# A two-block transformer kernel: small projection weights loaded by another queue, half of an early piece asked for sooner, router logits in two banks

## The reference

```
h = x + hybrid_mixer(rmsnorm(x), w_in, ...)          # delta rule heads, pooling, w_out
probs = softmax(rmsnorm(h) @ router_w)               # 16 experts
gate, idx = top_k(probs.T, 32)                       # each expert picks 32 tokens
h = h + scatter_add(gate * ((silu(xg @ w_gate[e]) * (xg @ w_up[e])) @ w_down[e]))
x2 = rmsnorm(h, norm_final)                          # end of block one
proj = rmsnorm(x2, norm_mix_2) @ w_in_2              # block two
(qa, ka, va, q_idx, k_idx, w_idx, qb, kb, vb, gdown, ogate) = split(proj)
   # sizes 512 512 512 256 32 8 256 256 512 16 512
x3 = x2 + concat(sparse_attention(...), gated_linear_attention(...)) @ w_out_2
y  = rmsnorm(x3 + ffn(rmsnorm(x3)))
```

## Time and profile before

| | |
|---|---|
| median of 3 runs | 1424.22 us (1423.8 to 1425.07) |
| the profiled execution | 1424.23 us |
| its span, first to last instruction | 1422.4 us |
| mean granted TensorE clock | 0.899 of full |
| HBM read | 475.88 MB, 335 GB/s over the span |
| TensorE, DVE, ACT, POOL busy | 77%, 26%, 22%, 22% |

### The profile page before, as it was taken

How to read it: one execution, slowest core, us unless ns; L and a number is a source line. 1 busy time by engine, 2 the same in 40 slices (tenths; PEclk the granted TensorE clock), 3 DMA queues, 4 the chain that set the end, 5 groups by cost and what they waited for, 6 DMA issues and landing times.

```text
span 1422.4 us, 19705 instructions
## 1 busy us (share of the span) xinstructions
PE 1092.7 (77%) x8358; PEld 629.3 (44%) x8358; DVE 369.9 (26%) x755; ACT 305.9 (22%) x457; POOL 307.7 (22%) x216
## 2 busy tenths in 40 slices
PE   7999997556756656666575665666678999999998
PEld 7998732111211211211031121121125988999997
DVE  6586530000100001000010010000104857553333
ACT  5753210000000000000000000000004636454443
POOL 6796000000000000000000000000003785386661
PEclk9999999888877888888888888888899999999999
DMA  9513999999999999999999999999999832575540
GB/s 288 186 34 121 389 425 428 427 428 427 428 428 428 429 428 428 429 428 429 428 428 429 429 428 428 428 429 427 428 428 330 220 119 92 178 249 178 178 149 30
DMA packets 95288, 478.06 MB, mean 336 GB/s; under 512 B 11098, under 2 KB 64217, under 8 KB 70393
## 3 DMA queue, kind: packets, MB, share of 16 engines
q1 hardware_dynamic: 94528, 476.30, 83.2%
q10 hardware_dynamic: 697, 0.84, 0.2%
HBM read 475.88 MB, written 1.25 MB: 335 GB/s over the span
## 4 chain that ended last, share of the span: by engine, by line
DMA 57%; PE 40%; DVE 2%; ACT 1%; issue 0%; SPq 0%; DVEq 0%; ACTq 0%
PE bank L1321 21%; DMA ring<-in_expert_w_down 20%; DMA ring<-in_expert_w_up 18%; DMA ring<-in_expert_w_gate 18%; PE bank L1024 4%; PE bank L2113 4%; PE bank L1046 2%; PE bank L410 1%; PE bank L427 1%; DMA ring<-in_w_in 1%; PE bank L1061 1%; PE bank L423 1%; PE bank L1515 0%; PE bank L1496 0%; PE bank L442 0%
## 5 line engine op out<-in xcount | busy, mean ns | idle before, releaser
L1024 PE MATMUL bank<-ring,work 128*32 128x512 f32 x2000 | 306.2, 745 | 201.6 <-DMA ring<-in_expert_w_up 124.4
L1024 PEld LDWEIGHTS bank<-ring,work 128*32 128x32 f32 x2000 | 60.5, 123 | 435.6 <-DMA ring<-in_expert_w_up 200.4
L1295 POOL TENSOR_TENSOR slot_r<-ring,slot_r 128x512 fp32r<-128x512 f32 (+1 forms) x123 | 226.8, 1873 | 102.5 <-ACT slot_r L1267 102.4
L1304 POOL TENSOR_TENSOR slot_r<-ring,slot_r 128x512 fp32r<-128x512 f32 x16 | 21.9, 1392 | 956.3 <-ACT slot_r L1273 956.3
L1046 PE MATMUL bank<-ring,work 128*32 128x512 f32 x1024 | 155.3, 741 | 85.8 <-DMA ring<-in_expert_w_down 81.0
L1321 PE MATMUL bank<-slot_r 128*128 128x256 f32 (+2 forms) x1080 | 160.5, 288 | 3.8 <-DVE tokm_r L2475 1.8
L1321 PEld LDWEIGHTS bank<-slot_r 128*128 128x128 f32 (+1 forms) x1080 | 145.2, 192 | 8.0 <-issue 5.3
L1098 DVE TENSOR_TENSOR work<-work,bank 128x512 f32<-128x512 f32 x16 | 11.0, 688 | 491.2 <-PE bank L1024 491.2
L1321 PE MATMUL bank<-work_r,slot_r 128*128 128x256 f32 x704 | 129.1, 283 | 0.2 <-DVE chan_r L1836 0.2
L1108 DVE SCALAR_TENSOR_TENSOR hres<-bank,work,hres 128x512 f32<-128x512 f32 x64 | 48.1, 751 | 276.0 <-PE bank L1061 272.8
L1267 ACT ACTIVATE slot_r<-ring 128x2048 fp32r<-128x2048 f32 x62 | 116.7, 1904 | 3.2 <-DMA ring<-in_w_in 3.2
(11 more groups left out here) (419 smaller groups left out, 1046.6 us busy)
## 6 DMA issues: line engine op xcount, KB each, us to landing
ring<-in_expert_w_down SPq DMA_DIRECT2D x64, 2048.0 KB, 35.7
ring<-in_expert_w_gate SPq DMA_DIRECT2D x63, 2048.0 KB, 36.0
ring<-in_expert_w_up SPq DMA_DIRECT2D x62, 2048.0 KB, 35.8
ring<-in_w_in SPq DMA_DIRECT2D x23, 1024.0 KB, 8.2
ring<-in_w_ffn_gate SPq DMA_DIRECT2D x11, 1024.0 KB, 5.7
ring<-in_w_ffn_up SPq DMA_DIRECT2D x11, 1024.0 KB, 5.4
ring<-in_w_ffn_down SPq DMA_DIRECT2D x11, 1024.0 KB, 4.9
ring<-in_w_out SPq DMA_DIRECT2D x8, 1024.0 KB, 5.0
```

The source lines that it names most:

```text
L1024: ins = pe.matmul(bank[b][32 * j:32 * j + 32, :], xg[:, 2 * s + kk, a * CAP:(a + 1) * CAP], w_[kk][:, j * W5:(j + 1) * W5], start=(s == 0 ...
L1295: ins = eng.tensor_tensor(ring_r[s][:, a:a + step], ring[:, s, a:a + step], ring_r[s][:, a + UNIT:a + UNIT + step].bitcast(F32), ALU.subtract)
L1304: ins = eng.tensor_tensor(ring_r[s][:, at:at + q], ring[:, s, at:at + q], ring_r[s][:, at + UNIT:at + UNIT + q].bitcast(F32), ALU.subtract)
```

## The change

Four edits:

1. The three loads of the small weights leave `second_sync` and slot 7. ACT issues them, in the last pair at its first expert (a = 0, expert 14), after that expert's gate products are done and ahead of its Silu (`small_weights`, signal `rel_in`). They go into `work0`. ACT makes `kgw_hi` and DVE `kgw_lo` in expert 15, between hT and the copies to `yo`; ACT waits for the loads there (`rel_in` 80), DVE for ACT (`act_chain` 4). SP no longer waits for them ahead of the bias rows. Two Square scratch places move, since `kgw` now lies in `work0`.
2. The `masks` half of the mask piece is issued right after pieces 2 and 3 instead of behind piece 5; the `work0` half stays where it was.
3. The logits of token tile t go into bank 2 or 5, with a signal each; DVE takes the maximum and its scaling for each tile by itself, and ACT's first Exp waits for the first tile's alone.
4. Counts of `SLOT_LOADS` and `ROUTED` follow.

```diff
-SLOT_LOADS["ffn"] = [n + m for n, m in zip(SLOT_LOADS["second"], (3, 3, 3, 3, 3, 2, 0, 19))]
+SLOT_LOADS["ffn"] = [n + m for n, m in zip(SLOT_LOADS["second"], (3, 3, 3, 3, 3, 2, 0, 16))]
...
-                    ins = pe.matmul(bank[2][:, t * E:(t + 1) * E], chan[:, k, t * P:(t + 1) * P], rw[:, k, :],
+                    ins = pe.matmul(bank[LOGITS[t]][:, 0:E], chan[:, k, t * P:(t + 1) * P], rw[:, k, :],
                                     start=(k == 0), stop=(k == DK - 1))
-            ins.then_inc(S.route_out, 1)
+                ins.then_inc(S.route_out, 1)
...
-                act.wait_ge(S.lmax_ready, 2)
+                act.wait_ge(S.lmax_ready, t + 1)
...
-            link(dve.tensor_reduce(lmax, bank[2][:, 0:TT * E].rearrange("p (t e) -> p t e", t=TT), AX.X, ALU.max))
-            dve.scalar_tensor_tensor(lmax, lmax, -1.0, rs, ALU.mult, ALU.mult).then_inc(S.lmax_ready, 2)
+            for t, done in enumerate(("first", "logits")):
+                dve.wait_ge(S.route_out, ROUTED[done])
+                link(dve.tensor_reduce(lmax[:, t:t + 1], bank[LOGITS[t]][:, 0:E], AX.X, ALU.max))
+                dve.scalar_tensor_tensor(lmax[:, t:t + 1], lmax[:, t:t + 1], -1.0, rs[:, t:t + 1], ALU.mult, ALU.mult)\
+                    .then_inc(S.lmax_ready, 1)
...
             for a in range(PAIR):
                 act.wait_ge(S.slot_used, SPE * (PAIR * i + a) + 4)
+                if last and a == 0:
+                    small_weights(act)
                 act.activation(sg, bank[GB][:, :], ACT.Silu).then_inc(S.silu_ready, 1)
...
                 if last and a == PAIR - 1:
                     act.activation(warm, eps, ACT.Sqrt)
+                    act.wait_ge(S.rel_in, 80)
+                    act.activation(kgw_hi, kgw_w, ACT.Copy).then_inc(S.act_chain, 1)
...
+        def small_weights(act):
+            w3 = io["w_in_2"].rearrange("o (k p) c -> (o p) k c", p=P)
+            for at, c, w in ((0, KI, IDX_DIM), (IDX_DIM, GD, GATE_RANK), (IDX_DIM + GATE_RANK, WI, IDX_HEADS)):
+                act.dma_start(kgw_w[:, :, at:at + w], w3[:, :, c:c + w]).then_inc(S.rel_in, 16)
...
                 if last and a == PAIR - 1:
+                    dve.wait_ge(S.act_chain, 4)
+                    dve.tensor_tensor(kgw_lo, kgw_w, kgw_hi.bitcast(F32), ALU.subtract).then_inc(S.chan_ready, 1)
                     dve.wait_ge(S.slot_used, SPE * E)
...
             for n in freed:
                 sp.wait_ge(*freed[n])
                 load_slot(sp, 0, n)
+                if n == 3:
+                    load_slot(sp, 0, MASK_PIECE, True)
...
-kgw_w = ring[:, 7, 3072:3072 + DK * KGW].rearrange("p (k c) -> p k c", k=DK)
-kgw_lo, kgw_hi = (ring_r[7][:, 3072 + i * DK * KGW:3072 + (i + 1) * DK * KGW].rearrange("p (k c) -> p k c", k=DK)
-                  for i in range(2))
+kgw_w = work0[:, 11 * W5:11 * W5 + DK * KGW].rearrange("p (k c) -> p k c", k=DK)
+kgw_lo, kgw_hi = (work0_r[:, a * W5:a * W5 + DK * KGW].rearrange("p (k c) -> p k c", k=DK) for a in (11, 4))
...
-                if n == 0:
-                    for at, c, w in ((0, KI, IDX_DIM), (IDX_DIM, GD, GATE_RANK), (IDX_DIM + GATE_RANK, WI, IDX_HEADS)):
-                        sp.dma_start(kgw_w[:, :, at:at + w], w3[:, :, c:c + w]).then_inc(slot_in[7], 16)
             sp.wait_ge(S.slot_used, total)
-            sp.wait_ge(slot_in[7], landed(7, "second", 3))
...
-            act.wait_ge(slot_in[7], landed(7, "second", 3))
-            act.activation(kgw_hi, kgw_w, ACT.Copy).then_inc(S.act_chain, 1)
...
-            dve.wait_ge(S.act_chain, 4)
-            dve.tensor_tensor(kgw_lo, kgw_w, kgw_hi.bitcast(F32), ALU.subtract).then_inc(S.chan_ready, 1)
```

More of the change, by code:

```diff
@@ L779, in build @@
         sems("spread_ready sel_ready idx_cols_ready")
-        ROUTED = {"logits": 1, "probT": 2, "places": 3, "idx_col": 4}
+        ROUTED = {"first": 1, "logits": 2, "probT": 3, "places": 4, "idx_col": 5}
+        LOGITS = (2, 5)
         rw = wab[:, :, :]
@@ L903, in route_act @@
             for t in range(TT):
-                act.wait_ge(S.lmax_ready, 2)
-                act.activation(lexp[:, t], bank[2][:, t * E:(t + 1) * E], ACT.Exp, bias=lmax[:, t:t + 1], scale=rs[:, t:t + 1],
+                act.wait_ge(S.lmax_ready, t + 1)
+                act.activation(lexp[:, t], bank[LOGITS[t]][:, 0:E], ACT.Exp, bias=lmax[:, t:t + 1], scale=rs[:, t:t + 1],
                                accum_out=lsum[:, t:t + 1]).then_inc(S.prob_exp, 1)
@@ L918, in route_dve @@
             dve.wait_ge(S.rms_ready, RMS["h1"] + TT)
-            dve.wait_ge(S.route_out, ROUTED["logits"])
-            link(dve.tensor_reduce(lmax, bank[2][:, 0:TT * E].rearrange("p (t e) -> p t e", t=TT), AX.X, ALU.max))
-            dve.scalar_tensor_tensor(lmax, lmax, -1.0, rs, ALU.mult, ALU.mult).then_inc(S.lmax_ready, 2)
+            for t, done in enumerate(("first", "logits")):
[3 more added lines that the diff above has]
+                    .then_inc(S.lmax_ready, 1)
             dve.wait_ge(S.prob_exp, TT)
@@ L1113, in build, with load_slot @@
         wd3 = io["expert_w_down"]
-        def load_slot(sp, i, n):
+        def load_slot(sp, i, n, masks_only=False):
             a, m = n // SPE, n % SPE
@@ L1125, in load_slot @@
             if isinstance(i, int) and n == MASK_PIECE:
-                sp.dma_start(work0[:, 8 * W5:12 * W5], piece[:, 0]).then_inc(S.pool_in, 16)
-                sp.dma_start(masks, piece[:, 1]).then_inc(S.pool_in, 16)
+                if not masks_only:
+                    sp.dma_start(work0[:, 8 * W5:12 * W5], piece[:, 0]).then_inc(S.pool_in, 16)
+                else:
+                    sp.dma_start(masks, piece[:, 1]).then_inc(S.pool_in, 16)
             elif isinstance(i, int) and n == ROUTE_PIECE:
@@ L1664, in second_act @@
                     act.wait_ge(S.sumsq_ready, SUMSQ["h2"] + 1)
-                act.activation(work0[:, (3 + 2 * t) * W5:(5 + 2 * t) * W5], tokm[:, t], ACT.Square, accum_out=ss2[:, t:t + 1])\
+                act.activation(chan[:, 4:8].rearrange("p k t -> p (k t)") if t else work0[:, 5 * W5:7 * W5], tokm[:, t], ACT.Square, accum_out=ss2[:, t:t + 1])\
                     .then_inc(S.act_chain, 1)
@@ L1806, in biases @@
                         pool.wait_ge(S.mask_ready, u // 8 + 1)
-                        pool.wait_ge(slot_in[7], landed(7, "second", 3 + TT * P // COPIES))
+                        pool.wait_ge(slot_in[7], landed(7, "second", TT * P // COPIES))
                     if u >= 2:
```

## The result

| | before | changed |
|---|---|---|
| median | 1424.22 us (21 runs) | 1426.12 us (21 runs, 1424.39 to 1428.51) |
| ratio of the runs | | 1.0015, 95% interval 1.0009 to 1.0021 |
| span of the profiled execution | 1422.4 us | 1425.4 us |

The change costs 1.9 us, 0.15%. The interval of the ratio lies wholly above 1, and the loss is smaller than the 0.2% at which the prediction drew its line: 1426.6 was forecast. The profiled execution of the changed kernel took 1427.17, about 1 us above its median.

What follows compares the result with a forecast made beforehand. The 16 DMA engines were taken to bound the kernel during the expert stream. +3.9 (small loads on ACT's queue) - 1.5 (removal after the experts) + 0 + 0 = +2.4: 1426.6 us; overall range 1421.8 to 1431.

Steps and rivals of the forecast that it cites:

- Bound and head: Expert stream: full DMA engines set the pace; start of kernel: early masks half and logits in two banks each worth 0.
- The dip at 151 to 154: Before the early piece: the moved masks half only lengthens the DMA dip, near 153 to 156, to twice as long.
- The step read from the store of rel_rows: Expert stream: an engine takes one packet of each queue in turn, whatever its size; one small packet per 0.62 us.
- rival A: Small loads are in before 1067, so no stall; -1.5 to +1.2 us, 1424 us; chance 0.16.
- Landing of the small weights: After the expert stream: the third small load, issued on ACT's queue at 985, lands at about 1085.2.
- Length of the stream: Expert stream: small packets move its end out by 148 x 0.011 = 1.6 us, from 1080.2 to 1081.8.
- Stall ahead of the scatter: After the last piece: waiting for the small loads starts the scatter near 1087.2 instead of 1083.06, +4.1 us including 1.6 longer stream.
- The gap won: Before the small products: TensorE's 1.54 us wait for kgw_lo goes; taken as 1.5 us gain, since TensorE comes later and POOL does not.
- The forecast's other end: After the experts: the next DVE operation takes kgw_lo's place beside POOL, leaving a gain of only 0.9 us.
- Silu of expert 14: Expert 14: ACT held at issue 12 to 37 us, TensorE may stand up to 20 us, engines don't starve; cost 0.
- rival B: ACT or SyncE held at issue, expert 14's Silu up to 1069, engines stand until about 1075: +10 to +31 us; chance 0.15.
- C: Early masks half moves the whole stream up by 2.45 us, with small loads in before 1067: 1421 us; chance 0.09.

Runs made afterwards that it cites:

- experiment 1: Kernel before plus early masks half and logits in two banks, together, then masks alone, then logits alone: ratios to before 0.9993, 0.9998 and 1.0001.
- experiment 2: Kernel before plus only the small-weights edits (loads on ACT's queue, both splits under expert 15), masks and logits as before: 1426.46 us, ratio 1.0015.
- experiment 4: Changed kernel with the small loads issued one wait earlier on ACT: ratio to before 1.0005; separately, with two small loads instead of three: 1.0007.
- reordered kernel: Kernel before plus masks and logits, kgw_lo ahead of DVE's norm operations, token tile 1's square sum on ACT, loads on SyncE: 1422.95, again 1422.28 us.

## Why the prediction was right

**Bound and head.** The stream is the bound, and masks and logits were taken as worth 0: right as far as experiment 1 can tell. The dip at 151 to 154 grew, as said.

**Small packets beside the stream.** The step read from the store of rel_rows, one packet of each queue in turn, was right: 52 against 52, and equal in steps of 0.2 us. The Trainium skill (DMA: Bandwidth & Descriptors, Queues, rings and completion order) says that an engine drains a whole packet of typically 9 to 17 descriptors from one queue before it switches. For these loads the steps of 0.2 us show no such batches, and rival A, which followed from the page's rule, is out: the measured counts decide. The "under 15 us" that the prediction drew from the rule would also need SyncE's turns to be single packets; with batches of both queues in turn the totals would be much the same as with single ones. ACT was held by the third load alone, for 34.9 us (forecast 12 to 37), until 936 of the 3,120 packets on its queue were through. (Each of the three loads adds 16 packets to the 3,072 that the prediction counted.)

**Landing of the small weights.** The third load landed 100.1 us after ACT began to issue; the forecast had 100.0. That it is so near is in part luck, because two sizes were wrong the opposite way. The turns were shorter than 0.62 us: from 1004 to 1008 us 114 packets of each queue went through 16 engines, one per 0.56 us, since SyncE's 114 moved only 1.69 MB, so that some 103 of them can have been of 16 KB. By 1081.6 therefore 3,046 of the 3,120 were through, 190 per engine, and not 148 of 192. But the last 74 still took 2.4 us, where the forecast gave 3.4 us to 44 on each engine. Why so few took so long is open; the profile does not tell the engines apart.

**Length of the stream.** Taken with 148 x 0.011 = 1.6 us. Measured 1.9 to 2.3 with three loads (four profiles), 1.6 and 1.9 with two. The count was too low, the price was right: from 984 to 1081.6 us the 3,046 packets took 2.2% of 16 engines' time, which is 2.1 us per engine and 0.011 us per packet. In the kernel with two loads ACT's queue took 1.7% of 984 to 1082, 1.7 us. Between 1030 and 1050 the engines moved 421 GB/s, where they moved 428 before.

**Stall ahead of the scatter.** Taken with some 2.5 us beside the stream's length. Measured 1.5 to 1.6 (4.4 from the last piece's first product to the scatter, before 2.8). Over-sized by 0.9: the steps from the landing to the scatter took the 2.0 us of the forecast, but the loads landed 2.4 us after the last piece and not 3.4, because ACT came to their issue 1.3 us sooner (983.91, taken with 985.19).

**The gap won.** Taken with 1.5, because TensorE would come later and POOL would not. Measured 1.7 (14.7 instead of 16.4 from scatter to broadcast, experiment 2). The premise was half right: in experiment 2 POOL's pair of operations came 1.8 us later too (1095.32 against 1093.55), but the scatter 2.8. The margin was thin: the reciprocal was ready 0.1 us before TensorE asked for it. The forecast's other end, that the next DVE operation takes the place of `kgw_lo` beside POOL, happened there as well, and cost time once the stall was gone (experiment 4): 0.5 us won. The Trainium skill (SBUF — State Buffer, Who interferes with whom) says that a VectorE operation with two inputs in SBUF contends with a GpSimd operation that reads SBUF; the trace agrees with 3.81 us for the square sum, which reads `hres` twice, beside POOL's split and 1.21 without it.

**Silu of expert 14.** It came at 1020 instead of 985, TensorE stood 16.8 us, and the engines moved 418 to 425 GB/s between 1030 and 1050: no hole. Right, and rival B is out. C is out with experiment 1.

**Sum.** +2.0 (stream) + 1.55 (stall) - 1.7 (gap) = +1.9 us; forecast +2.4, measured +1.9. So the mechanism was right, and the sum came out near partly because the stream was taken too short by 0.3 to 0.7 us and the stall too long by 0.9. What the prediction did not name is the low clock in the scatter, 1.7 us in the changed kernel's profile. It is no part of this sum and, by experiment 2, not of every execution. The median seems to need none of it: the early piece's issue as before (153.8), a stream of 928.3, a hand-over of 19.1 and 323.0 behind it make 1424.2, and the median less the 1.8 us around the span is 1424.3. That is worked out from single profiles and not shown.

**A wrong reading without effect.** The prediction called the expert weights and their products three quarters of the chain of waits. The page's shares (20, 18, 18, 4, 2 and 1%) add up to 63%.

## What to carry to other kernels

A load costs the bound engine by its packets as well as by its bytes, and on a second queue beside a full stream of big packets it got one packet through for each big one here: count the packets per engine, multiply by the big packet's time, and compare with the time until someone needs it. The issuing engine can be held too, here by the third load of 64 packets per engine. Before a wait is paid for with work in the bound stage, look whether reordering what stands around it removes it; and after it is removed, look which operation now meets the neighbour that had made the old one slow.

## What the runs showed of the hardware that was not expected

- After an idle stretch of 1.8 us TensorE ran at its lower clock for some 3.4 us of the scatter (5.37 us for 8 products instead of 3.67) in one profile, and at full clock after the same 1.84 us in another. From 1030 us to the stall the granted clock was 1.00 in both, and TensorE's busy time was nearly the same.
- ACT, held at the issue of the third load, was let go when 928 to 946 of the 3,120 packets on its queue were through (four profiles), that is with some 136 per engine left. The prediction had worked out the same number for SyncE.
- The head of the kernel, up to the issue at 154 us, drifts by up to 3 us between executions (on several chips) of kernels that do the same there. Differences below 1 us in the whole span of two profiles say nothing. The stream of the seven kernels without small packets in it agrees within 0.4 us; the hand-over was 19.24 us in all four kernels that leave it as it was, but 17.7 and 18.3 in two profiles of the same reordered kernel.
